# Values of the two dilated groups with tokens stationary, in a two-layer decoder trunk

## What is computed

```
def shared_kv(x, kv_norm, w_kv):
    h = rms_norm(x, kv_norm)
    kv = (h @ w_kv).reshape(B, S, 2, N_DGROUPS, N_HEADS, HEAD_DIM)
    k = rotary(kv[:, :, 0])
    v = kv[:, :, 1]
    return [(key_blocks(k[:, :, g], dil), key_blocks(v[:, :, g], dil))
            for g, (_, dil) in enumerate(DILATED_GROUPS)]
```

## Time and profile before

| what | value |
|---|---|
| median of 3 runs | 1481.43 us (1480.38 to 1485.12) |
| profiled execution, its own time | 1482.62 us |
| its span, first to last instruction | 1480.8 us |
| mean granted TensorE clock | 0.984 |
| TensorE busy | 1420.7 us, 96% |
| VectorE busy | 1128.1 us, 76% |
| ScalarE busy | 785.9 us, 53% |
| GpSimd busy | 457.8 us, 31% |
| chain that ended last, TensorE's share | 87% |

### The profile page before, as it was taken

The page is one execution under the profiler, slowest core; times in us unless marked ns, Lnnn a source line. Parts: engine busy times, 40 slices in busy tenths (PEclk is TensorE's granted clock), DMA queues, the critical chain, the costliest instruction groups (busy, mean ns, idle before and its releaser), DMA issues.

```text
span 1480.8 us, 20665 instructions
## 1 busy us (share of the span) xinstructions
PE 1420.7 (96%) x7296; PEld 1156.7 (78%) x7296; DVE 1128.1 (76%) x1647; ACT 785.9 (53%) x1024; POOL 457.8 (31%) x330
## 2 busy tenths in 40 slices
PE   7999997999999997999999999999998899999997
PEld 5889685788888865888888888888887588888863
DVE  6999728888888869766858667585753888888866
ACT  5211835777777736344252533424353677777733
POOL 0000014344444410422405133150402544444310
PEclk9999997999999999999999999999999999999999
DMA  5242516899999954222212122131546599999872
GB/s 218 86 135 90 213 54 258 324 373 380 383 385 393 373 220 179 91 71 71 85 57 99 57 85 71 57 99 57 197 142 239 203 357 378 383 386 376 324 316 107
DMA packets 52765, 309.87 MB, mean 209 GB/s; under 512 B 10544, under 2 KB 16432, under 8 KB 38896
## 3 DMA queue, kind: packets, MB, share of 16 engines
q1 hardware_dynamic: 42128, 291.48, 51.3%
q0 software_dynamic: 9792, 16.80, 3.1%
q10 hardware_dynamic: 800, 1.00, 0.2%
HBM read 299.27 MB, written 28.84 MB: 222 GB/s over the span
## 4 chain that ended last, share of the span: by engine, by line
PE 87%; DVE 6%; DMA 2%; ACT 2%; issue 2%; POOL 0%; SPq 0%; DVEq 0%; POOLq 0%; ACTq 0%
PE PS L2185 5%; PE PS L2186 5%; PE PS L2187 5%; PE PS L2039 4%; PE PS L2038 4%; PE PS L2042 4%; PE PS L2025 4%; PE PS L2026 4%; PE PS L2027 4%; PE PS L2074 3%; PE PS L2075 3%; PE PS L2078 3%; PE PS L2201 3%; PE PS L2203 3%; PE PS L2202 3%; PE PS L2063 2%
## 5 line engine op out<-in xcount | busy, mean ns | idle before, releaser
L832 POOL TENSOR_TENSOR KQ<-rope_ab 64x512 f32<-64x512 f32 x96 | 173.6, 1809 | 316.5 <-DVE rope_ab L1698 312.9
L1573 DVE TENSOR_TENSOR wgl<-WR,wgh 128x2048 fp32r<-128x2048 f32 x66 | 150.9, 2293 | 39.3 <-ACT wgh L999 39.3
L1110 ACT ACTIVATE wh<-wraw 128x1024 fp32r<-128x1024 f32 x76 | 80.3, 1058 | 174.3 <-PE PS L2187 170.0
L1573 DVE TENSOR_TENSOR wul<-WR,wuh 128x2048 fp32r<-128x2048 f32 x66 | 148.4, 2288 | 5.2 <-issue 5.2
L1620 DVE TENSOR_TENSOR wdl<-WR,wdh 128x2048 fp32r<-128x2048 f32 x56 | 128.2, 2289 | 25.8 <-ACT wdh L1032 25.8
L1698 DVE TENSOR_TENSOR rope_ab<-PS,rope_sb 32x512 f32<-32x512 f32 x192 | 131.9, 687 | 2.6
L999 ACT ACTIVATE wuh<-WR 128x2048 fp32r<-128x2048 f32 x66 | 122.8, 1908 | 10.9 <-PE PS L2027 10.9
L1032 ACT ACTIVATE wdh<-WR 128x2048 fp32r<-128x2048 f32 x56 | 107.4, 1919 | 36.6 <-PE PS L2078 36.6
L999 ACT ACTIVATE wgh<-WR 128x2048 fp32r<-128x2048 f32 x66 | 125.1, 1903 | 0.0
L1680 DVE TENSOR_TENSOR wl<-wraw,wh 128x1024 fp32r<-128x1024 f32 x76 | 94.6, 1245 | 31.6 <-ACT wh L1110 30.1
L2038 PE MATMUL PS<-wgh,xgh 128*128 128x512 f32 x264 | 108.7, 412 | 1.4 <-ACT xgh L1015 1.4
(11 more groups left out here) (371 smaller groups left out, 3519.9 us busy)
## 6 DMA issues: line engine op xcount, KB each, us to landing
WR<-w_gate SPq DMA_DIRECT2D x33, 2048.0 KB, 12.0
WR<-w_up SPq DMA_DIRECT2D x33, 2048.0 KB, 9.3
WR<-w_down SPq DMA_DIRECT2D x33, 2048.0 KB, 12.0
wraw<-w_qkv SPq DMA_DIRECT2D x72, 512.0 KB, 3.3
WR<-w_in SPq DMA_DIRECT2D x8, 1024.0 KB, 4.9
xn_dram<-SC SPq DMA_DIRECT2D x8, 512.0 KB, 2.8
SC<-y_dram SPq DMA_DIRECT2D x8, 512.0 KB, 6.0
HT<-y_dram SPq DMA_DIRECT2D x8, 512.0 KB, 9.2
```

Of the source, the lines that this page charges most:

```text
L832: nc.gpsimd.tensor_tensor(to, cos, sin, ALU.add).then_inc(rope_done, 1)
L1573: V.tensor_tensor(lo[:, kts, :], raw[:, kts, :], hi[:, kts, :].bitcast(F32), ALU.subtract).then_inc(done, 1)
```

## The change

The near group keeps its way: weights stationary, then turned. For the two dilated groups the roles are changed. A set of 128 tokens (every fourth) is stationary, from `HTh` or `HTl`, and the weight tiles of both groups move side by side, 128 + 128 = 256 columns. The result has tokens on the partitions and both groups' values in the row; four of them fill two banks, PS3 (sets 0 and 1) and PS2 (sets 2 and 3). ScalarE stores each bank once, with a reordering access pattern. The copy to `vT`, the four transposes and the store are gone for both groups. Both weight slots stay in use to the end of the fourth token set, so `lead(7)` moves on ScalarE behind the last store and `trailing(1)` moves on VectorE behind two copies. The counter bases follow.

```diff
-                    if g == 0:
-                        pe.wait_ge(pairs_done, i + 1)
-                    if g == 2:
+                def dilated_values(n, kts=range(KT)):
+
+                    if n == 0 and kts[0] == 0:
+                        pe.wait_ge(wl_done, 9 * i + 9)
+                    if n == 2:
                         pe.wait_ge(v_done, 3 * i + 1)
-                    dst = PS[2 + g % 2][:, :]
+                    dst = PS[3 - n // 2][:, 256 * (n % 2):256 * (n % 2) + 256]
                     for kt in kts:
-                        whk, wlk = wh[:, g, kt * P:(kt + 1) * P], wl[:, g, kt * P:(kt + 1) * P]
-                        M.matmul(dst, whk, HTh[:, kt, :], start=kt == 0, stop=False)
-                        M.matmul(dst, whk, HTl[:, kt, :], start=False, stop=False)
-                        ins = M.matmul(dst, wlk, HTh[:, kt, :], start=False, stop=kt == KT - 1)
...
+                        hi, lo = HTh[:, kt, tile_of(1, n)], HTl[:, kt, tile_of(1, n)]
+                        wh_k, wl_k = wh[:, 1:NU, kt * P:(kt + 1) * P], wl[:, 1:NU, kt * P:(kt + 1) * P]
+                        M.matmul(dst, hi, wh_k, start=kt == 0, stop=False)
+                        M.matmul(dst, hi, wl_k, start=False, stop=False)
+                        ins = M.matmul(dst, lo, wh_k, start=False, stop=kt == KT - 1)
+                    if n == 1 and kts[-1] == KT - 1:
+                        ins.then_inc(v_mm, 1)
+                    if n == NT - 1:
+                        ins.then_inc(unit_mm, 2)
...
-                values(0)
-                values(1, range(3))
+                near_values()
+                dilated_values(0, range(6))
                 scores(0)
-                turn(0)
-                values(1, range(3, KT))
+                turn_near()
+                dilated_values(0, range(6, KT))
+                dilated_values(1)
                 swap(0)
                 scores(1)
-                values(2, range(KT // 2))
+                dilated_values(2)
                 turn_weights(0, 0)
                 turn_weights(0, 1)
-                turn(1)
-                values(2, range(KT // 2, KT))
+                dilated_values(3)
                 swap(1)
                 turn_weights(0, 2)
                 turn_weights(0, 3)
-                turn(2)
                 meanwhile(i)
```

ScalarE's part (`store_near_values` is the old `store_values` for group 0):

```diff
+                def store_dilated_values(first):
+
+                    if first == 0:
+                        act.wait_ge(v_mm, 2 * i + 2)
+                    else:
+                        act.wait_ge(unit_mm, 9 * i + 9)
+                    nc.scalar.activation(Vs[:, 1:NG, first:first + 2, :, :].rearrange("p g n h d -> p n g (h d)"),
+                                         PS[3 - first // 2][:, :].rearrange("p (n g x) -> p n g x", n=2, g=2), ACT.Copy).then_inc(v_done, 1)
...
-                copy_values(0)
+                copy_near_values()
                 lead(6)
-                store_values(0)
-                copy_values(1)
+                store_near_values()
                 for side in (1, 0):
                     weights(0, side)
-                lead(7)
                 copy_turned(0, 0)
                 copy_turned(0, 1)
-                store_values(1)
+                store_dilated_values(0)
...
-                copy_values(2)
-                weights(1, 1, range(2))
-                store_values(2)
-                weights(1, 1, range(2, NT))
-                weights(1, 0)
+                store_dilated_values(2)
+                lead(7)
+                for side in (1, 0):
+                    weights(1, side)
                 lead(8)
```

More of the change, by code:

```diff
@@ L500, in build_program @@
         dl_done = [Later(bout_added, NT), Later(oTl_done, KT)]
-        down_half = [Later(yph_done, len(BY_BANDS)), Later(vT_done, 3 * NP_HEADS)]
+        down_half = [Later(yph_done, len(BY_BANDS)), Later(vT_done, NP_HEADS)]
         y_added, y_cleared = Later(taps_done, len(BY_TAPS)), Later(sem("y_cleared"), 0)
@@ L1114, in pair_act, with copy_near_values, store_near_values @@
             def pair_act(i):
[L1115 to L1125, removed]
-                                         ACT.Copy).then_inc(v_done, 1)
+                def copy_near_values():
+                    act.wait_ge(unit_mm, 9 * i + 7)
+                    nc.scalar.activation(vT[:, :], PS[2][:, :], ACT.Copy).then_inc(vT_done, 1)
+                def store_near_values():
+                    act.wait_ge(v_mm, 2 * i + 1)
+                    nc.scalar.activation(Vs[:, 0, :, :, :], PS[2][:, :].rearrange("p (n h d) -> p n h d", n=NT, h=2),
+                                         ACT.Copy).then_inc(v_done, 1)
+                def store_dilated_values(first):
[5 more added lines that the diff above has]
+                                         PS[3 - first // 2][:, :].rearrange("p (n g x) -> p n g x", n=2, g=2), ACT.Copy).then_inc(v_done, 1)
                 def lead(u):
@@ L1734, in pair_dve @@
                 maxima(1)
-                trailing(1, 9 * i + (7 + NU + 1))
                 if isinstance(i, int):
@@ L1743, in pair_dve @@
                 copy_turned(0, 3)
+                trailing(1, 9 * i + (7 + NU + 1))
                 dve.wait_ge(exp_done, 16 * i + 16)
@@ L2188, in pair_pe, with near_values @@
                     ins.then_inc(unit_mm, 1)
-                def values(g, kts=range(KT)):
-                    if kts[0] == 0:
-                        pe.wait_ge(wl_done, 9 * i + (7 + g))
-                    if g == 0:
-                        pe.wait_ge(pairs_done, i + 1)
-                    if g == 2:
+                def near_values():
+                    pe.wait_ge(wl_done, 9 * i + 7)
+                    pe.wait_ge(pairs_done, i + 1)
+                    for kt in range(KT):
+                        whk, wlk = wh[:, 0, kt * P:(kt + 1) * P], wl[:, 0, kt * P:(kt + 1) * P]
+                        M.matmul(PS[2][:, :], whk, HTh[:, kt, :], start=kt == 0, stop=False)
+                        M.matmul(PS[2][:, :], whk, HTl[:, kt, :], start=False, stop=False)
+                        ins = M.matmul(PS[2][:, :], wlk, HTh[:, kt, :], start=False, stop=kt == KT - 1)
+                    ins.then_inc(unit_mm, 1)
@@ L2197, in values, with turn_near @@
+                def turn_near():
+                    pe.wait_ge(vT_done, i + 1)
+                    for n in range(NT):
+                        ins = M.transpose(PS[2][:, n * P:(n + 1) * P], vT[:, tile_of(0, n)], ident[:, :])
+                    ins.then_inc(v_mm, 1)
[3 more added lines that the diff above has]
+                    if n == 2:
                         pe.wait_ge(v_done, 3 * i + 1)
-                    dst = PS[2 + g % 2][:, :]
+                    dst = PS[3 - n // 2][:, 256 * (n % 2):256 * (n % 2) + 256]
```

## The result

The changed kernel takes 1567.05 us (median of 4 runs, 1565.79 to 1568.54) against 1482.39 us before in the same comparison: a ratio of 1.057, 95% interval 1.0549 to 1.0591. It is slower by 85 us, far outside the range of 1474 to 1493.

The account below looks back on a forecast made before the run. TensorE, busy 96% of the span, was taken to bound the kernel. Seven pairs at -0.10 us gave -0.7, the last pair +0.6, in sum -0.1 us: 1481.3 us in terms of the median, range 1474 to 1493.

Parts of the forecast that it names:

- 96x - 11.72 per pair: TensorE, pair loop: 96 new matmuls at spacing x replace 10.92 us of value matmuls and 0.80 us of turnings.
- x: TensorE: start-to-start spacing of the new 256-column dilated matmuls, forecast at 121 ns, with break-even at 122 ns.
- the third bound: Stationary load with stride 4, read from the turnings: some 11 ns more than contiguous, a spacing floor of 120 ns.
- the two readings: Dilated matmul spacing: fixed price per matmul (121 ns) and strided floor (120 ns), taken as independent and not adding.
- a fixed price of 14 ns: Dilated matmuls: each costs 14 ns besides its columns whatever their number, so 107 + 14 = 121 ns.
- The upper bound: Dilated matmuls: if the load did not hide beside a 107 ns matmul, spacing would be the load's duration, 207 ns.
- Rival 1: Dilated matmuls: cost besides columns grows with the columns, spacing 114 ns, 5.5 us faster, 1475.9 us; chance 0.24.
- Rival 2: Dilated matmuls: strided load slows the stream by 11 ns, spacing 132 ns, 8.3 us slower, 1489.7 us; chance 0.27.
- rival 3: Dilated matmuls: the load does not hide, spacing 207 ns, +8.15 us a pair, about +65, 1546 us; chance 0.05.
- The covers: ScalarE, VectorE and SP work moved in the pair loop: forecast cost 0, with 1 us and 0.17 us to spare.
- The last pair's wait for its weights: TensorE, last pair: waits some 0.8 us for the moved weight tile's trailing part; this pair ends about 0.6 us later.
- 0.80 us for the turnings: TensorE, each pair: two of the three turnings go, 0.40 us each, saving 0.80 us.

Follow-up runs that it names:

- the neighbours' run: The changed kernel with 128 neighbouring tokens stationary in the dilated matmuls instead of every fourth one: 1479.22 us, ratio 0.9989 to the kernel before.

## Why the prediction was wrong, point by point

- **Where the time would be decided.** Right: TensorE alone, in the pair loop, with no new wait; the change of the time is 96x - 11.72 per pair, and x is the distance of starts in a run of dilated matmuls.
- **x.** The failed step is the third bound, "a strided load costs some 11 ns more and has a floor of 120 ns", with what hangs on it, that the two readings "run side by side, so they do not add". The floor was read from four transposes. A matmul with this stride has a load pace of 233 ns, at 128, 256 and nearly unchanged at 512 columns, in rounded and in full precision. Those two readings agreed on 120 to 121 by coincidence, and I took the agreement for support. The other half of the estimate, a fixed price of 14 ns, was right: with neighbours x is 120.
- **The upper bound.** I put 207 ns there, the duration of a strided load in a transpose. It was too low even as a bound, by 26 ns. And I gave the case that the load does not hide 0.05, arguing that loads overlap their neighbours. They do; but the load is itself the slower stream, and overlapping does not help that.
- **The Trainium skill** ("SBUF — State Buffer", Door 1: The DMA port swizzle, the note on cachelines) was the rule that spoke against the change, and its sentence on two hits in a line agrees with the loads: two elements in 16 bytes give full speed (196 ns at stride 2), one does not (329 at stride 4, 339 at stride 8). The same note adds that one can stride for free as far as 4 elements of fp32; if that means a stride of 4, the 233 ns speak against it. I let the transposes' 120 ns overrule it instead of making it a rival with its full price. For moving operands the rule is not enough: two hits with a jump after them cost 340 ns instead of 227.
- **Rivals.** Rival 1 is refuted by the neighbours' run: 120 ns, not 114. Rival 2 and rival 3 had the direction right and the strided load as the cause, but neither the size nor the way. Rival 2 let the load add 11 ns to the stream, and beside 512 columns it adds 8, while beside 256 it adds 113 and beside 128 it still stands at 233: that is a maximum and no sum. Rival 3, +8.15 us a pair, came nearest to the measured +10.43, with a load that does not hide; in fact loads of 329 ns overlap, at a pace of 233.
- **The covers.** ScalarE's moved conversion, the earlier due time of the third tile (0.17 us to spare) and SP's later refill cost nothing: no wait stands in the repeated part. In the changed kernel the longer pair gives each of them more room than was forecast; the neighbours' run, with a pair of 63.07 us and no such wait either, is the proper test. The last pair's wait for its weights came, 0.7 us for 0.8.
- **0.80 us for the turnings** is about right: with x = 120 the formula gives -0.20 us a pair, measured is -0.40. The difference lies at the borders of the blocks, which the formula leaves out.

## What to carry to other kernels

Before a stationary and a moving operand change places, look at how many elements of the new stationary one lie in 16 bytes. Here, with 4-byte elements, two were free; with one, the load set the pace up to 256 columns, and halving the columns gave nothing back. Do not price an access pattern from transposes: take it from a matmul, or measure it. Where a stride must be, an order of storage with a stride of 2 costs nothing to load, provided that everything that moves can still be read as it lies.

## What the runs showed of the hardware that I had not expected

- A matmul's load of 128 columns has a pace of 233 ns at a stride of 4 elements of 4 bytes, the same at both granted clocks, and of 241 ns at a stride of 8; with neighbours or a stride of 2 the matmuls of 256 columns go at 120 ns. Transposes with a stride of 4 go at 120 too.
- Moving operands pay too: 512 columns in 458 ns with stride 4, in 340 ns in pairs with jumps, in 227 ns as stored.
- TensorE can be covered with rows all the time and still be granted the lower clock: in the one run with strided loads and 128 rounded columns a stretch of 6 us stood at 0.50 in the middle of a pair, and the mean over the program was 0.925 instead of 0.985. What brings it about is open.
